# Placement of short extra matmuls in TensorE's stream, in a two-block transformer kernel

## The chip, the cores and the metric

The kernel runs on one core of one Trainium2 chip. The metric is the device time of one execution in microseconds (us). The core's engines are TensorE (PE, matmuls), VectorE (DVE), ScalarE (ACT), GpSimd (POOL) and SyncE (SP, which issues the loads). "PEld" in a profile is TensorE's weight load, which overlaps its matmuls.

## The reference

256 tokens of width 1024, everything in float32. Two blocks of two layers each, run one after the other:

- first block: a layer with MLA attention (16 heads) and one with an mLSTM mixer (4 heads), each followed by a squared-ReLU MLP of width 4096;
- second block: in each of two layers a SwiGLU MLP of width 2816, a mixer (a gated short convolution in the first, sparse attention with compressed, selected and windowed keys in the second), and a second SwiGLU MLP.

```python
for i in range(DEPTH):                      # first block, DEPTH = 2
    hn = rms_norm(x, norm_mix[i])
    y = mla_mixer(hn, ...) if i == 0 else mlstm_mixer(hn, ...)
    x = x + y
    x = x + sqrelu_mlp(rms_norm(x, norm_ffn[i]), ffn_w1[i], ffn_w2[i])
for i in range(DEPTH):                      # second block
    if i == 1: kv = shared_kv(h, ...)
    h = h + 0.5 * swiglu_ffn(rmsnorm(h, ffn1_norm[i]), ffn1_w_in[i], ffn1_w_out[i])
    hn = rmsnorm(h, mix_norm[i])
    h = h + (short_conv_mixer(hn, ...) if i == 0 else nsa_mixer(hn, ..., kv))
    h = h + 0.5 * swiglu_ffn(rmsnorm(h, ffn2_norm[i]), ffn2_w_in[i], ffn2_w_out[i])
```

## The kernel before, in words

All weights are a stream of 518 tiles of 128x1024 (512 KB). A tile comes by DMA into one of four buffers `raw`, ScalarE rounds it to `w_hi` (L551), VectorE subtracts to get the rest, `w_lo` (L1018), and TensorE multiplies. The buffers go round: SP loads a tile into a buffer when VectorE has split the one before it.

Activations are split into high and low parts too and lie in `xs`, `hs` or `os`, features on the partitions and the 256 tokens beside one another. A product of one 128x128 weight chunk with one 128x256 activation chunk is therefore three matmuls into one PSUM bank, which `narrow_product` issues: L1731 (`w_hi` by high), L1732 (`w_hi` by low) and L1735 (`w_lo` by high). One weight tile holds eight such chunks, so a tile is 24 matmuls.

The stages come in this order: MLA with its output projection wo_a; up_0, down_0; mLSTM (mgate, mqk, mv, mo) and wo_m; up_1, down_1; glu_0, out_0; cin, cout; glu_1, out_1; kv and kvc; glu_2, out_2; the sparse attention (nq, ngate) and wo_n; glu_3, out_3.

- `feature` makes the stages dq, dkv, kr, mqk, kvc, up_*, glu_* and cin: one output of 128 features for each weight tile, eight chunks deep. Where `norm_` is given, `two` computes outputs 0 and 1 together, chunk by chunk, with the row sums of the norm (`sums`, L1750, L1753) ahead of the last chunk. Then come a head of outputs written out singly, with what `between` asks for behind some of them, and a rolled loop of eight outputs at a time.
- `residual` makes down_* (32 outputs of `up`, four tiles an output) and out_* (22 chunks, three tiles an output): output `o`, tile `j`, chunk `c`. It reads `hs`.
- `residual_one` makes wo_a, wo_m, cout and wo_n.

`odd_matmul` (L1724) multiplies a constant 128x128 matrix in plain float32 with 60 columns of ones, into the last columns of bank 7 that nobody reads. The profile shows it as two records of L1724. Its result is used nowhere. In the kernel before, up_0, up_1 and glu_3 (`odds=3`) issue three of them in output 2: inside the product of chunk 0 (between L1732 and L1735), behind chunk 2 and behind chunk 4. glu_0, cin and glu_1 (`odds=1`) issue one, behind the pair of outputs 0 and 1. Everything else issues none. The compression in glu_2 has one real matmul of the same form, `compressed_sums` (L2062), behind output 15.

Of the kernel before, what the change touches and what calls it, by code (L numbers as in the profile page):

```python
# [30 lines left out]
P = 128  # L31
# [3 lines left out]
KD = D // P  # L35
BLK = 8
TILE = BLK * P
RING = 4
# [13 lines left out]
FF1 = 4096 // P  # L52
FF2 = 2816 // P
# [83 lines left out]
def build(nc, x_in, tiles, vecs, rows, consts, rel_bias, w1c_k, w1c_v, w2c_k, w2c_v, y_out):  # L137
    ctx = ExitStack()
    with ctx:
        def sb(name, shape, dt=F32):  # L140
            return ctx.enter_context(nc.sbuf_tensor(name, shape, dt))
# [38 lines left out]
        xs = sb("xs", [P, KD * 2 * S], F32R)  # L180
# [10 lines left out]
        def bank(b, a=0, z=BANK, p=slice(None)):  # L191
            return psum[p, b * BANK + a:b * BANK + z]

        def const(name, a, z, p=slice(None)):
            at = CONST[name]
            return con[p, at + a:at + z]
# [1524 lines left out]
        def _(pe):  # L1721
            def odd_matmul(b=7):

                pe.matmul(bank(b, 448, 508), const("blockdiag", 0, P), ones[:, 0:60], start=True, stop=True)  # L1724

            def narrow_product(out_bank, lhs, k, src, first, last, inside=None):

                s, c = lhs
                x_hi, x_lo = src[:, k * 2 * S:k * 2 * S + S], src[:, k * 2 * S + S:(k + 1) * 2 * S]
                out = bank(out_bank, 0, S)  # L1730
                pe.matmul(out, w_hi[s][:, c:c + P], x_hi, start=first, stop=False)  # L1731
                pe.matmul(out, w_hi[s][:, c:c + P], x_lo, start=False, stop=False)  # L1732
                if inside:
                    inside()
                return pe.matmul(out, w_lo[s][:, c:c + P], x_hi, start=False, stop=last)  # L1735
# [17 lines left out]
                            ins = pe.matmul(bank(STAT, tb, tb + 1), ssq[:, tb * P:(tb + 1) * P], ones[:, 0:1], start=True, stop=True)  # L1753
                ins.then_inc(stat_done, 1)

            def feature(name, outs, xs_name, src=xs, norm_=None, between=None, norm_at=0, odds=0):


                between = between or {}
                t0, o0 = TILE0[name], OUT0[name]  # L1760

                def one(u, i=0, wait_x=False):
                    s, b = (t0 + u) % RING, (o0 + u) % 4
                    pe.wait_ge(lo_ready, i * 4 + (t0 + u + 1))
                    if not (isinstance(i, int) and o0 + u + 4 * i < 4):
                        pe.wait_ge(out_read, i * 4 + (o0 + u - 3))
                    for k in range(KD):
                        if wait_x:
                            pe.wait_ge(xs_ready, XS0[xs_name] + k + 1)
                        more = odds == 3 and u == 2 and isinstance(i, int) and i == 0  # L1770
                        ins = narrow_product(b, (s, k * P), k, src, k == 0, k == KD - 1, odd_matmul if more and k == 0 else None)
                        if more and k in (2, 4):
                            odd_matmul()
                    ins.then_inc(tile_done, 1)

                def two():

                    pe.wait_ge(lo_ready, t0 + 2)
                    pe.wait_ge(out_read, o0 + 1 - 3)
                    for k in range(KD):  # L1780
                        pe.wait_ge(xs_ready, XS0[xs_name] + k + 1)
                        if norm_ and k == KD - 1:
                            sums(norm_)
                        for u in range(2):
                            ins = narrow_product((o0 + u) % 4, ((t0 + u) % RING, k * P), k, src, k == 0, k == KD - 1)
                            if k == KD - 1:
                                ins.then_inc(tile_done, 1)

                head = outs if outs < 16 else outs % 8 or 8
                while head <= max([*between, 2 if odds else 0]):  # L1790
                    head += 8
                paired = norm_ is not None and outs > 1 and name != "dq"
                if paired:
                    two()
                if odds == 1:
                    odd_matmul()
                for u in range(2 if paired else 0, head):
                    one(u, 0, u == 0)
                    if u in between:
                        between[u]()  # L1800
                    if norm_ and not paired and u == norm_at:
                        sums(norm_)
                if head < outs:
                    with pe.Fori(0, (outs - head) // 8) as i:
                        for u in range(8):
                            one(head + u, i * 2)

            def residual(name, per, chunks, src, ready):

                t0, o0 = TILE0[name], OUT0[name]  # L1810
                for o in range(KD):
                    pe.wait_ge(out_read, o0 + o - 3)
                    for j in range(per):
                        t = t0 + o * per + j
                        pe.wait_ge(lo_ready, t + 1)
                        for k in range(min(BLK, chunks - j * BLK)):
                            c = j * BLK + k
                            if o == 0:
                                pe.wait_ge(*ready(c))
                            ins = narrow_product((o0 + o) % 4, (t % RING, k * P), c, src, c == 0, c == chunks - 1)  # L1820
                        ins.then_inc(tile_done, 1)

            def residual_one(name, src, ready, between=None):


                between = between or {}
                t0, o0 = TILE0[name], OUT0[name]

                def chunk(o, c):
                    if c == 0:  # L1830
                        pe.wait_ge(out_read, o0 + o - 3)
                        pe.wait_ge(lo_ready, t0 + o + 1)
                    ins = narrow_product((o0 + o) % 4, ((t0 + o) % RING, c * P), c, src, c == 0, c == KD - 1)
                    if c == KD - 1:
                        ins.then_inc(tile_done, 1)

                for c in range(KD):
                    pe.wait_ge(*ready(max(c, 1) if name == "wo_a" else c))
                    chunk(0, c)
                    chunk(1, c)  # L1840
                    if c in between:
                        between[c]()
                for o in range(2, KD):
                    for c in range(KD):
                        chunk(o, c)
# [177 lines left out]
            def swap_rows(o):  # L2023

                pe.wait_ge(c_flat_, o + 1)
                if o >= 2:
                    pe.wait_ge(c_swapped, o - 1)
                pe.matmul(bank(6 + o % 2, 0, S), c_turned_rows, c_flat[o], start=True, stop=True).then_inc(c_swap, 1)
# [182 lines left out]
            def warm(n, b=7):  # L2211

                for _ in range(n):
# [3 lines left out]
            warm(24)  # L2217
            mla()
            residual_one("wo_a", os_, after(xs_ready, XS0["o_a"]), {0: lambda: turn_outputs("o_a", o_tok, (a_o, H - 1), [6]), 1: lambda: turn_outputs("o_a", o_tok, (a_o, H), [7])})
            feature("up_0", FF1, "ffn_0", norm_="ffn_0", odds=3)  # L2220
            residual("down_0", FF1 // BLK, FF1, hs, after(hs_ready, hid0["up_0"]))
            mlstm()
            residual_one("wo_m", os_, after(xs_ready, XS0["o_m"]),
                         {3: lambda: turn_outputs("o_m", m_h, (m_gated, 2), [4, 5, 6]),
                          4: lambda: turn_outputs("o_m", m_h, (m_gated, 2), [7])})
            feature("up_1", FF1, "ffn_1", norm_="ffn_1", odds=3)
            residual("down_1", FF1 // BLK, FF1, hs, after(hs_ready, hid0["up_1"]))
            feature("glu_0", 2 * FF2, "pre_0", norm_="pre_0", odds=1)
            residual("out_0", FF2_TILES, FF2, hs, after(hs_ready, hid0["glu_0"]))
            feature("cin", 3 * KD, "mid_0", norm_="mid_0", odds=1)  # L2230
            residual_one("cout", hs, after(hs_ready, hid0["cin"]))
            feature("glu_1", 2 * FF2, "post_0", norm_="post_0", odds=1)
            residual("out_1", FF2_TILES, FF2, hs, after(hs_ready, hid0["glu_1"]))
            nsa_kv()
            feature("glu_2", 2 * FF2, "pre_1", os_, between={2: lambda: swap_rows(3), 6: keys_turned, 10: compress, 13: compressed, 15: compressed_sums})
            residual("out_2", FF2_TILES, FF2, hs, after(hs_ready, hid0["glu_2"]))
            nsa()
            residual_one("wo_n", os_, after(xs_ready, XS0["o_n"]), {c: lambda c=c: turn_outputs("o_n", no_tok, (n_oo, 1), [c + 4]) for c in range(KD - 4)})
            feature("glu_3", 2 * FF2, "post_1", norm_="post_1", odds=3)
            residual("out_3", FF2_TILES, FF2, hs, after(hs_ready, hid0["glu_3"]))  # L2240


# [105 lines left out]
```

## Time and profile before

| | |
|---|---|
| time, median of 3 runs | 1556.84 us (1556.03 to 1557.47) |
| the profiled execution | 1556.84 us, span of the trace 1555.1 us |
| PE busy | 1541.5 us, 99% |
| DVE busy, ACT busy | 1041.9 us (67%), 849.8 us (55%) |
| granted TensorE clock | 1.00 over the span |
| HBM read | 278 MB, 180 GB/s |

Matmuls are pipelined: one lasts longer in the trace than the time from its start to the next start, so a busy PE may run at different paces. The start times of the timeline are in us from the start of the span; L1731 and so on are lines of the kernel. A window's count (x) includes instructions that overlap its edges.

### The profile page before, as it was taken

To read this page: it belongs to the slowest core of one execution; us is meant where nothing else is said; L and a number is where in the kernel's file an instruction comes from. 1 tells how busy PE (TensorE), PEld (TensorE's weight loads), DVE (VectorE), ACT (ScalarE), POOL (GpSimd) and SP (SyncE) were. 2 spreads that over 40 slices of the span, in tenths; PEclk is the share of its full clock that TensorE was granted. 3 is DMA by queue.
4 is the path that set the end of the run, shared out by engine and by line. 5 is a ranking of instruction groups with operands and counts; after the bars stand their busy time and mean duration, and the time that the engine had idled before them with its cause. 6 is when DMAs were issued, how large, how long until landed. Compare 5 with 4: busy or idle time off the path is not lost.

```text
span 1555.1 us, 35183 instructions
## 1 busy us (share of the span) xinstructions
PE 1541.5 (99%) x12856; PEld 1502.0 (97%) x12856; DVE 1041.9 (67%) x1751; ACT 849.8 (55%) x1301; POOL 124.1 (8%) x123
## 2 busy tenths in 40 slices
PE   9999999999999999999999999999999999999999
PEld 8899999988999999999999999989999988999999
DVE  7677765643876557666787766678576656676664
ACT  6776554546665445445445555556555547655543
POOL 1830000036000000000000000000000032200000
PEclk9999999999999999999999999999999999999999
DMA  7246666554566566666666666656566981065564
GB/s 242 71 123 193 197 192 197 169 168 148 183 194 197 188 199 190 195 193 202 193 204 191 200 191 192 211 179 208 188 192 195 229 210 55 15 203 190 192 201 149
DMA packets 80784, 281.02 MB, mean 181 GB/s; under 512 B 8880, under 2 KB 12464, under 8 KB 80688
## 3 DMA queue, kind: packets, MB, share of 16 engines
q1 hardware_dynamic: 76800, 274.78, 56.2%
q10 hardware_dynamic: 3888, 4.85, 1.7%
q8 instruction: 73, 1.20, 0.3%
q14 instruction: 23, 0.19, 0.0%
HBM read 278.03 MB, written 1.57 MB: 180 GB/s over the span
## 4 chain that ended last, share of the span: by engine, by line
PE 93%; DVE 4%; DMA 2%; ACT 1%; issue 1%; SPq 0%; DVEq 0%; ACTq 0%
PE psum L1731 27%; PE psum L1735 27%; PE psum L1732 27%; DMA raw<-tiles 2%; PE psum L1862 2%; PE psum L1864 2%; PE psum L1863 2%; PE psum L2151 1%; PE psum L2102 1%; DVE w_lo L1018 1%; PE psum L2135 1%; PE psum L2049 0%; ACT w_hi L551 0%; PE psum L1926 0%; PE psum L1916 0%
## 5 line engine op out<-in xcount | busy, mean ns | idle before, releaser
L551 ACT ACTIVATE w_hi<-raw 128x1024 fp32r<-128x1024 f32 x518 | 547.1, 1058 | 483.1 <-PE psum L1735 423.6
L1018 DVE TENSOR_TENSOR w_lo<-raw,w_hi 128x1024 fp32r<-128x1024 f32 x484 | 592.2, 1224 | 247.7 <-ACT w_hi L551 247.1
L1731 PE MATMUL psum<-xs,w_hi 128*128 128x256 f32 x1928 | 535.8, 278 | 2.1 <-DVE w_lo L1018 2.1
L1735 PE MATMUL psum<-xs,w_lo 128*128 128x256 f32 x1928 | 533.0, 276 | 0.0
L1732 PE MATMUL psum<-xs,w_hi 128*128 128x256 f32 x1928 | 532.8, 276 | 0.0
L1731 PEld LDWEIGHTS psum<-xs,w_hi 128*128 128x128 f32 x1928 | 361.9, 188 | 3.1 <-DVE w_lo L1018 2.5
L1732 PEld LDWEIGHTS psum<-xs,w_hi 128*128 128x128 f32 x1928 | 361.9, 188 | 0.3
L1735 PEld LDWEIGHTS psum<-xs,w_lo 128*128 128x128 f32 x1928 | 361.8, 188 | 0.0
L1735 PE MATMUL psum<-hs,w_lo 128*128 128x256 f32 x1280 | 353.3, 276 | 0.0
L1731 PE MATMUL psum<-hs,w_hi 128*128 128x256 f32 x1280 | 353.3, 276 | 0.0
L1732 PE MATMUL psum<-hs,w_hi 128*128 128x256 f32 x1280 | 353.3, 276 | 0.0
L1731 PEld LDWEIGHTS psum<-hs,w_hi 128*128 128x128 f32 x1280 | 240.2, 188 | 0.0
L1735 PEld LDWEIGHTS psum<-hs,w_lo 128*128 128x128 f32 x1280 | 240.2, 188 | 0.0
L1732 PEld LDWEIGHTS psum<-hs,w_hi 128*128 128x128 f32 x1280 | 240.2, 188 | 0.0
L471 POOL TENSOR_TENSOR w_lo<-raw,w_hi 128x1024 fp32r<-128x1024 f32 x34 | 81.7, 2412 | 1175.5 <-ACT w_hi L551 1175.5
L1731 PE MATMUL psum<-os,w_hi 128*128 128x256 f32 x544 | 152.8, 281 | 0.6 <-DVE os L1212 0.6
L1732 PE MATMUL psum<-os,w_hi 128*128 128x256 f32 x544 | 151.3, 278 | 0.0
L1735 PE MATMUL psum<-os,w_lo 128*128 128x256 f32 x544 | 151.2, 278 | 0.0
L1731 PEld LDWEIGHTS psum<-os,w_hi 128*128 128x128 f32 x544 | 102.1, 188 | 1.1 <-DVE os L1212 0.9
L1732 PEld LDWEIGHTS psum<-os,w_hi 128*128 128x128 f32 x544 | 102.2, 188 | 0.1
L1735 PEld LDWEIGHTS psum<-os,w_lo 128*128 128x128 f32 x544 | 102.0, 187 | 0.0
L1041 DVE SCALAR_TENSOR_TENSOR xs<-x,vec,xs 128x256 fp32r<-128x256 f32 (+1 forms) x80 | 38.1, 482 | 54.0 <-ACT xs L565 54.0
(284 smaller groups left out, 1464.9 us busy)
## 6 DMA issues: line engine op xcount, KB each, us to landing
raw<-tiles SPq DMA_DIRECT2D x518, 512.0 KB, 4.3
bias<-bias_dram ACTq DMA_DIRECT2D x8, 256.0 KB, 8.6
x<-x_in SPq DMA_DIRECT2D x4, 256.0 KB, 5.2
w1c_all<-w1c_k ACTq DMA_DIRECT2D x4, 256.0 KB, 4.3
w1c_all<-w1c_v ACTq DMA_DIRECT2D x4, 256.0 KB, 5.8
y_out<-x SPq DMA_DIRECT2D x8, 128.0 KB, 3.5
con<-consts SPq DMA_DIRECT2D x1, 771.0 KB, 8.9
bias_dram<-bias_row ACTq DMA_DIRECT2D x1, 512.0 KB, 7.1
```

Of the source, the lines that this page charges most:

```text
L471: pool.tensor_tensor(w_lo[s][:, :], raw[s][:, :], w_hi[s][:, :].bitcast(F32), ALU.subtract).then_inc(lo_ready, 1)
L551: act.activation(w_hi[s][:, :], raw[s][:, :], ACT.Copy).then_inc(hi_ready, 1)
L1018: dve.tensor_tensor(w_lo[s][:, :], raw[s][:, :], hi_of(w_hi[s][:, :]), ALU.subtract).then_inc(lo_ready, 1)
L1041: dve.scalar_tensor_tensor(out=dst, in0=src, scalar=gain, in1=hi_of(hi), op0=ALU.mult, op1=ALU.subtract).then_inc(xs_ready, 1)
L1731: pe.matmul(out, w_hi[s][:, c:c + P], x_hi, start=first, stop=False)
L1732: pe.matmul(out, w_hi[s][:, c:c + P], x_lo, start=False, stop=False)
L1735: return pe.matmul(out, w_lo[s][:, c:c + P], x_hi, start=False, stop=last)
L1862: pe.matmul(out, x_hi, w_hi[s][:, col:col + 512], start=c == 0, stop=False)
L1863: pe.matmul(out, x_hi, w_lo[s][:, col:col + 512], start=False, stop=False)
L1864: ins = pe.matmul(out, x_lo, w_hi[s][:, col:col + 512], start=False, stop=c == chunks - 1)
L2102: return pe.matmul(bank(n_bank[2 * e + br], at_, at_ + k1), n_qTa[rows, k * S + q0:k * S + q1], kT[rows, key0:key0 + k1], start=True, stop ...
L2135: ins = pe.transpose(bank(4 + br, n * P, (n + 1) * P), n_p[e][:, col:col + P], ident)
```

## The change

The option `odds` of `feature` goes. In its place `inside` names a function to call within the product of chunk 4 of a given output (between L1732 and L1735), beside `between`, which calls one behind an output.

- up_0, up_1, glu_0, cin, glu_1 and glu_3: three short matmuls each, inside chunk 4 of output 2, behind output 2 and behind output 3.
- glu_2: three, in the same way, at outputs 16, 16 and 17, into bank 4.
- every `residual` stage (down_0, down_1, out_0 to out_3): three in output 0, inside the product of chunk 4, behind tile 0 and behind tile 1.

```diff
-            def feature(name, outs, xs_name, src=xs, norm_=None, between=None, norm_at=0, odds=0):
+            def feature(name, outs, xs_name, src=xs, norm_=None, between=None, norm_at=0, inside=None):
-                between = between or {}
+                between, inside = between or {}, inside or {}
...
-                        more = odds == 3 and u == 2 and isinstance(i, int) and i == 0
-                        ins = narrow_product(b, (s, k * P), k, src, k == 0, k == KD - 1, odd_matmul if more and k == 0 else None)
-                        if more and k in (2, 4):
-                            odd_matmul()
+                        ins = narrow_product(b, (s, k * P), k, src, k == 0, k == KD - 1, inside.get(u) if k == 4 else None)
...
-                while head <= max([*between, 2 if odds else 0]):
+                while head <= max(between, default=0):
                     head += 8
...
-                if odds == 1:
-                    odd_matmul()
...
-                            ins = narrow_product((o0 + o) % 4, (t % RING, k * P), c, src, c == 0, c == chunks - 1)
+                            ins = narrow_product((o0 + o) % 4, (t % RING, k * P), c, src, c == 0, c == chunks - 1,
+                                                 odd_matmul if (o, c) == (0, 4) else None)
                         ins.then_inc(tile_done, 1)
+                        if o == 0 and j < 2:
+                            odd_matmul()
...
-            feature("up_0", FF1, "ffn_0", norm_="ffn_0", odds=3)
+            feature("up_0", FF1, "ffn_0", norm_="ffn_0", between={2: odd_matmul, 3: odd_matmul}, inside={2: odd_matmul})
...
-            feature("glu_0", 2 * FF2, "pre_0", norm_="pre_0", odds=1)
+            feature("glu_0", 2 * FF2, "pre_0", norm_="pre_0", between={2: odd_matmul, 3: odd_matmul}, inside={2: odd_matmul})
...
-            feature("glu_2", 2 * FF2, "pre_1", os_, between={2: lambda: swap_rows(3), 6: keys_turned, 10: compress, 13: compressed, 15: compressed_sums})
+            feature("glu_2", 2 * FF2, "pre_1", os_, between={2: lambda: swap_rows(3), 6: keys_turned, 10: compress, 13: compressed, 15: compressed_sums, 16: lambda: odd_matmul(4), 17: lambda: odd_matmul(4)}, inside={16: lambda: odd_matmul(4)})
```

up_1 and glu_3 change like up_0, cin and glu_1 like glu_0.

## Rows read from the trace of the kernel before

**Rows 1.** The page: busy time of the engines, and the chain by engine.
```profile
PE 1541.5 (99%) x12856; PEld 1502.0 (97%) x12856; DVE 1041.9 (67%) x1751; ACT 849.8 (55%) x1301; POOL 124.1 (8%) x123
...
PE 93%; DVE 4%; DMA 2%; ACT 1%; issue 1%; SPq 0%; DVEq 0%; ACTq 0%
```

**Rows 2.** Waits of PE: us in total, times, longest.
```profile
PE psum L2096 <- DVE arena L1605: 2.2, 2, 1.9
PE psum L1731 <- DVE w_lo L1018: 2.1, 2, 1.6
```

**Rows 3.** Windows, PE alone: window, us, PE busy (count), granted clock, DMA share, GB/s.
```profile
101.00:123.00 22.00, 22.00 (x189) 1.00 0.65 168
130.00:290.00 160.00, 160.00 (x1414) 1.00 0.63 196
...
1125.00:1250.00 125.00, 125.00 (x1106) 1.00 0.74 206
...
1385.00:1545.00 160.00, 160.00 (x1414) 1.00 0.61 198
```

**Rows 4.** Line L1735 on `hs`, whole span: ns min/median/max, first and last start.
```profile
L1735 PE MATMUL psum<-hs,w_lo x1280: 276/276/278, 207.9 to 1551.7; 128*128 128x256 f32 x183
```

**Rows 5.** Timeline of PE in glu_0: start, duration (us).
```profile
587.60 0.28 PE L1735 MATMUL psum<-xs,w_lo 128*128 128x256 f32 x1
587.71 0.33 PE L1724 MATMUL psum<-ones,con 128*128 128x60 f32 x2
...
588.05 0.28 PE L1732 MATMUL psum<-xs,w_hi 128*128 128x256 f32 x1
```

**Rows 6.** Timeline of PE in up_0, output 2.
```profile
125.55 0.32 PE L1724 MATMUL psum<-ones,con 128*128 128x60 f32 x2
...
125.89 0.28 PE L1731 MATMUL psum<-xs,w_hi 128*128 128x256 f32 x1
...
126.46 0.28 PE L1735 MATMUL psum<-xs,w_lo 128*128 128x256 f32 x1
126.58 0.33 PE L1724 MATMUL psum<-ones,con 128*128 128x60 f32 x2
126.71 0.37 PE L1731 MATMUL psum<-xs,w_hi 128*128 128x256 f32 x1
126.92 0.28 PE L1732 MATMUL psum<-xs,w_hi 128*128 128x256 f32 x1
...
127.39 0.28 PE L1735 MATMUL psum<-xs,w_lo 128*128 128x256 f32 x1
```

**Rows 7.** Timeline of PE in glu_3, output 2.
```profile
1377.15 0.28 PE L1732 MATMUL psum<-xs,w_hi 128*128 128x256 f32 x1
...
1377.61 0.28 PE L1731 MATMUL psum<-xs,w_hi 128*128 128x256 f32 x1
...
1378.20 0.28 PE L1735 MATMUL psum<-xs,w_lo 128*128 128x256 f32 x1
...
1378.66 0.28 PE L1732 MATMUL psum<-xs,w_hi 128*128 128x256 f32 x1
...
1379.13 0.28 PE L1735 MATMUL psum<-xs,w_lo 128*128 128x256 f32 x1
...
1379.58 0.28 PE L1732 MATMUL psum<-xs,w_hi 128*128 128x256 f32 x1
```

**Rows 8.** Groups by line, 124.95 to 125.42 (up_0): busy us, mean ns.
```profile
L1735 PE MATMUL psum<-xs,w_lo 128*128 128x256 f32 x2 | 0.6, 280 | 0.0
```

**Rows 9.** Groups by line, 587.38 to 587.65 (glu_0).
```profile
L1731 PE MATMUL psum<-xs,w_hi 128*128 128x256 f32 x1 | 0.3, 280 | 0.0
```

**Rows 10.** Groups by line, 1376.65 to 1377.12 (glu_3, ahead of the first L1724).
```profile
L1731 PE MATMUL psum<-xs,w_hi 128*128 128x256 f32 x2 | 0.6, 280 | 0.0
```

**Rows 11.** Groups by line, 1377.86 to 1378.18 (glu_3, behind the first L1724).
```profile
L1735 PE MATMUL psum<-xs,w_lo 128*128 128x256 f32 x1 | 0.3, 280 | 0.0
```

**Rows 12.** Timeline of PE in glu_2, behind output 15.
```profile
1121.13 0.33 PE L2062 MATMUL psum<-arena,con 128*128 128x60 f32 x2
```

More of the change, by code:

```diff
@@ L2225, in _ @@
                           4: lambda: turn_outputs("o_m", m_h, (m_gated, 2), [7])})
-            feature("up_1", FF1, "ffn_1", norm_="ffn_1", odds=3)
+            feature("up_1", FF1, "ffn_1", norm_="ffn_1", between={2: odd_matmul, 3: odd_matmul}, inside={2: odd_matmul})
             residual("down_1", FF1 // BLK, FF1, hs, after(hs_ready, hid0["up_1"]))
-            feature("glu_0", 2 * FF2, "pre_0", norm_="pre_0", odds=1)
+            feature("glu_0", 2 * FF2, "pre_0", norm_="pre_0", between={2: odd_matmul, 3: odd_matmul}, inside={2: odd_matmul})
             residual("out_0", FF2_TILES, FF2, hs, after(hs_ready, hid0["glu_0"]))
-            feature("cin", 3 * KD, "mid_0", norm_="mid_0", odds=1)
+            feature("cin", 3 * KD, "mid_0", norm_="mid_0", between={2: odd_matmul, 3: odd_matmul}, inside={2: odd_matmul})
             residual_one("cout", hs, after(hs_ready, hid0["cin"]))
-            feature("glu_1", 2 * FF2, "post_0", norm_="post_0", odds=1)
+            feature("glu_1", 2 * FF2, "post_0", norm_="post_0", between={2: odd_matmul, 3: odd_matmul}, inside={2: odd_matmul})
             residual("out_1", FF2_TILES, FF2, hs, after(hs_ready, hid0["glu_1"]))
             nsa_kv()
-            feature("glu_2", 2 * FF2, "pre_1", os_, between={2: lambda: swap_rows(3), 6: keys_turned, 10: compress, 13: compressed, 15: compressed_sums})
+            feature("glu_2", 2 * FF2, "pre_1", os_, between={2: lambda: swap_rows(3), 6: keys_turned, 10: compress, 13: compressed, 15: compressed_sums, 16: lambda: odd_matmul(4), 17: lambda: odd_matmul(4)}, inside={16: lambda: odd_matmul(4)})
             residual("out_2", FF2_TILES, FF2, hs, after(hs_ready, hid0["glu_2"]))
@@ L2238, in _ @@
             residual_one("wo_n", os_, after(xs_ready, XS0["o_n"]), {c: lambda c=c: turn_outputs("o_n", no_tok, (n_oo, 1), [c + 4]) for c in range(KD - 4)})
-            feature("glu_3", 2 * FF2, "post_1", norm_="post_1", odds=3)
+            feature("glu_3", 2 * FF2, "post_1", norm_="post_1", between={2: odd_matmul, 3: odd_matmul}, inside={2: odd_matmul})
             residual("out_3", FF2_TILES, FF2, hs, after(hs_ready, hid0["glu_3"]))
```

## Prediction

> **What bounds the kernel now.** I read the page first. TensorE (PE) is busy for 1541.5 of 1555.1 us, VectorE for 67% and ScalarE for 55%, and 93% of the chain that ended last is PE [rows 1]. The view of waits says the same: the longest total wait of PE for another engine is 2.2 us, the one for a split weight tile 2.1 us [rows 2]. So PE's own stream sets the end; time added to it adds to the span, and nearly nothing beside it can hide it.
>
> But "busy" can't say how fast the stream runs. I therefore counted PE's matmuls in stretches that hold only the products of `narrow_product` (256 columns each). A row counts about two matmuls that straddle the edges of its window. From 130 to 290 us that gives 160/(1414-2) = 0.1133 us from one start to the next; from 101 to 123 us it gives 22/(189-2) = 0.1176 us [rows 3]. The granted clock is 1.00 in both, the level of 2.4 GHz. So the same instructions run at two paces, 0.0043 us (3.8%) apart. I call them fast and slow. Each has its own duration of one matmul as well: 276 ns when fast [rows 4], up to 280 ns when slow [rows 8 to 11]. From the end of the short matmuls of up_0 to the end of down_0, and likewise in up_1/down_1, glu_0/out_0, cin/cout, glu_1/out_1, the rest of glu_2/out_2 and glu_3/out_3, the pace is fast. In particular the 1280 matmuls of L1735 on `hs`, which are those of every `down`, `out` and `cout` stage, last 276 ns in the median and 278 at most [rows 4]: no such stage has a slow stretch today.
>
> **What a short matmul does, from the timeline.** The order in time around the existing short ones (L1724) shows that they switch the pace.
>
> - glu_0, one of them, between L1735 and the next L1731: slow before, fast after [rows 5].
> - up_0, three: after L1732 (slow to fast), after an L1735 (fast to slow), after an L1735 (slow to fast). The five steps from 125.89 to 126.46 take 0.114 each, the four from 126.92 to 127.39 0.1175 [rows 6].
> - glu_3, three at the same places: slow, slow, slow, and fast only after the third. The five steps from 1377.61 to 1378.20 still take 0.118, the four from 1378.66 to 1379.13 too; from 1385 us on the pace is 160/1412 = 0.1133 [rows 3, 7].
>
> So it is no plain toggle. In the slow pace one of the three matmuls of a product lasts 280 ns and the others a nanosecond or two less, and which one it is differs: L1735 ahead of up_0's first short matmul, L1731 ahead of the one in glu_0 and of glu_3's first, L1735 again after glu_3's first [rows 8 to 11]. All the cases fit one rule: if the 280 ns matmul is the one right behind the insertion, the pace becomes fast; otherwise it becomes slow (or stays so) with the 280 ns matmul moved to just behind the insertion. A 60-column matmul of the compression (L2062) did the same at 1121.13, so that glu_2 runs fast from its tile 16 on today: 125/1104 = 0.1132 [rows 3, 12].
>
> The new train is: inside chunk 4 (ahead of L1735), after the tile (ahead of L1731), after the next tile (ahead of L1731). By the rule it ends fast from every start: the first leaves "fast" or "280 at L1735", the second then always "280 at L1731", the third always "fast". I don't expect the change to lose the fast pace; it can't win it either, because every stage that it touches has it already, and the slow stretches (wo_a, mLSTM's projections, wo_m, kvc and the first 16 tiles of glu_2, wo_n) lie outside it or ahead of its trains.
>
> **The sum, from the profiled execution (1556.84 us, which is also the median of the runs).** What is left is the price.
>
> One short matmul: in glu_3, L1732 at 1377.15 to L1732 at 1379.58 is 2.43 us and holds 15 steps, three for each of five chunks [rows 7]. At 0.1176 they make 1.76, so the three cost 0.67 over the slow pace, 0.22 each. The one in glu_0 agrees: 588.05-587.60 = 0.45 for two steps, less 0.235 [rows 5]. The fast-to-slow one: 126.92-126.46 = 0.46, the same [rows 6].
>
> 1. Six residual stages (down_0, down_1, out_0 to out_3), all new: three short ones 0.67. Between the first and the last 34 matmuls (10 to the end of the first tile, 24 of the second) and the two steps spanning the last one turn slow: 36 x 0.0043 = 0.155. Together 0.82 each, 4.9 us.
> 2. glu_2, new, in a stretch that L2062 had made fast: same shape, 0.82.
> 3. glu_0, cin, glu_1: one short one becomes three (+0.45), and the pace turns fast two tiles later (48 x 0.0043 = 0.21): 0.66 each, 2.0 us.
> 4. up_0, up_1: three before and after, spread wider. Of the 50 steps behind the pair of tiles, 12 are slow before and 42 after: 30 x 0.0043 = 0.13 each, 0.26 us.
> 5. glu_3: 17 of the 50 slow before, all after: 33 x 0.0043 = 0.14 us.
>
> Sum 4.9 + 0.8 + 2.0 + 0.26 + 0.14 = 8.1 us, with 27 more short matmuls (39 for 12). 1556.84 + 8.1 = **1564.9 us**, 0.5% slower.
>
> The edits that I cost at nothing: the bank (4 or 7) and the `inside` plumbing, which issue nothing. DMA, VectorE and ScalarE get no new work, and their ring of four weight tiles is fed with slack (VectorE 67% busy). If that cover were gone, PE would wait at a tile start; a delay of PE only gives them more time. Conversely, up to the 2.1 us that PE waits for split tiles today [rows 2] could swallow some of the delay. That is the low bound: 1564.9 - 2.1 = 1562.8. What queues behind a short matmul is only the next product; the tile's release to the DMA ring comes 0.22 us later.
>
> What isn't seen before is an insertion inside a product while the pace is fast. Its price is bounded by the nearest rows: 0.22 and slow afterwards (as the other fast-to-slow one), or 0.22 and still fast for the 10 matmuls to the next one, which saves 7 x 10 x 0.0043 = 0.3 us. I take the first. Below nothing isn't possible where the pace is already fast.
>
> **The rivals.**
>
> *A (not slower): a short matmul pays only for its columns.* With the stream already fast, its two records of 60 columns might slip in at the pace of the others: 120/256 x 0.1133 = 0.053 us, 27 of them 1.4 us, with the pace kept: 1558.3 us, within 0.2%. It decides below 3.1/27 = 0.115 us for one. For it: two records start only 0.13 us before the product after them [rows 6]. Against it: in up_0 the one put into a fast stream took 0.46 for two steps like the others, twice the deciding price. Chance 0.04. The Trainium skill, page TensorE: Matmul & The Clock Gate, section "Wait — 56ns, not 53.3ns?", says that starts come no closer than about 25 ns however few the columns; an estimate from that page is 27 x 2 x 0.025 = 1.4 us, 1558.2 us.
>
> *B (slower, but by less): the new short matmuls cost their time and don't move the pace.* 27 x 0.22 = 6.0 us, 1562.8 us. Against it: up_0's second one made a fast stream slow [rows 6]; for it: none was seen inside a product of a fast stream. Chance 0.02. The Trainium skill, page TensorE: Matmul & The Clock Gate, same section, gives one start-to-start time at the full clock, N/2.4 plus about 2.5 ns, or 109 ns for 256 columns; by that rule an insertion never moves the pace, while the trace has two paces, 113.3 and 117.6 ns, at one granted clock.
>
> *C: a train that starts fast ends slow.* If inserting inside a product from the fast pace left the 280 ns matmul at L1731 rather than L1735, the second would give fast and the third slow. Then down_0 and down_1 run their other 718 matmuls slow (3.1 us each), the four out stages 478 each (2.1), glu_2's rest 624 (2.7): 6.2 + 8.4 + 2.7 = 17 us more, less out_2, which would then start slow and be mended: 15, or 1580 us. For it: this transition is in no row. Against it: the rule fits every one that is, and glu_3 shows that inside from slow leaves it at L1735. A plain toggle would give about the same time, and glu_3 speaks against it. Chance 0.05.
>
> *D: one or two stages only end slow*, because at some place the steps between the insertions are disturbed (a wait for a tile or a bank at the tile's boundary). 2.1 to 3.1 us each: 1567 to 1571 us. The one in glu_0 sits at such a boundary and works, as do those in cin and glu_1. Chance 0.05.
>
> *E: a train mends more than its own stage*, say mLSTM's projections or wo_n, which are slow now. After down_0 these are 46 tiles of 24 matmuls (mgate 2, mqk 8, wo_m 8, kvc 4, 16 of glu_2, wo_n 8), 1104 x 0.0043 = 4.7 us: 1560.2 at best, still slower. Against it: at each of them row sums or other fp32 work comes between. Chance 0.02.
>
> **How the numbers follow.** My forecast has 0.82: 1564.9, with a range of its own from 1562.8 (some delay swallowed) to 1566. A has 0.04, B 0.02, C 0.05, D 0.05, E 0.02. The range of 1562.5 to 1570 takes in the forecast, B and most of D, 0.88 or so. 0.2% is 3.1 us, about what a measurement of this kernel can tell from no change. Slower by more: forecast, B, C, D and E, 0.94 to 0.96; I say 0.94. Within: A and a little more absorption, 0.05. Faster: 0.01, for something that no row shows.
>
> **What the profile after would show.** 78 records of the short matmul in place of 24; in each residual stage the durations rise from 276 to up to 280 ns from chunk 4 to the end of chunk 15 of the first output and are back at 276 from then on; each of these stages 0.8 us longer; glu_2 0.8 us longer behind tile 16; glu_0, cin, glu_1 0.66 us longer; PE busy by about 8 us more; the median over the matmuls on `hs` still 276 ns. I am wrong if that median goes to 279 (C), if a short one costs under 0.12 us (A), if a new train leaves the pace as it is (B), or if unprofiled executions don't run at the paces of this profile.

## The result, and the profile after

The changed kernel takes 1565.29 us (1564.33 to 1567.98, 4 runs) against 1556.43 us for the kernel before (1555.81 to 1557.47, 4 runs): ratio 1.0057, 95% interval 1.0044 to 1.0069. It is 8.9 us slower; 8.1 were forecast. The profiled execution took 1565.57 us, its span is 1563.8 us.

The page of the changed kernel, the lines that answer to [rows 1]:

```profile
PE 1551.1 (99%) x12910; PEld 1511.7 (97%) x12910; DVE 1042.3 (67%) x1751; ACT 849.8 (54%) x1301; POOL 123.9 (8%) x123
...
PE 95%; DVE 3%; ACT 1%; issue 0%; DMA 0%; SPq 0%; ACTq 0%; DVEq 0%
```

PE is busy for 9.6 us more with 54 more matmul records; VectorE and ScalarE do what they did. The view of single lines (ns min/median/max) has the short matmuls, 78 records for 24, and L1735 on `hs`, which answers to [rows 4]:

```profile
L1724 PE MATMUL psum<-ones,con x78: 213/244/274, 126.8 to 1506.0; 128*128 128x60 f32 x78
```

```profile
L1735 PE MATMUL psum<-hs,w_lo x1280: 276/276/366, 207.9 to 1560.5; 128*128 128x256 f32 x183
```

The median is still 276 ns: the residual stages are fast except close to their trains. Only the maximum is new, the matmul right behind an insertion. (An insertion is one short matmul, a train the two or three that stand together.) Windows of PE in the changed kernel, behind the trains of up_0, down_0 and out_3, read as [rows 3]:

```profile
130.00:205.00 75.00, 75.00 (x664) 1.00 0.64 201
215.00:299.00 84.00, 84.00 (x743) 1.00 0.60 193
...
1507.00:1560.00 53.00, 53.00 (x471) 1.00 0.53 175
```

75/662 = 0.1133, 84/741 = 0.1134 and 53/469 = 0.1130 us: the fast pace, within a matmul or two of the count. The timeline of PE around the third insertion of down_0's train shows the return to it:

```profile
213.58 0.28 PE L1735 MATMUL psum<-hs,w_lo 128*128 128x256 f32 x1
213.70 0.33 PE L1724 MATMUL psum<-ones,con 128*128 128x60 f32 x2
...
214.04 0.28 PE L1732 MATMUL psum<-hs,w_hi 128*128 128x256 f32 x1
214.15 0.28 PE L1735 MATMUL psum<-hs,w_lo 128*128 128x256 f32 x1
214.26 0.28 PE L1731 MATMUL psum<-hs,w_hi 128*128 128x256 f32 x1
```

From 213.58 to 214.04 are two steps of 0.46 in all, as in [rows 5 to 7], and then 0.11 each.

The norms' row sums (L1750) are marks to measure stages by: they stand ahead of the last chunk of the first pair of outputs, so 42 product matmuls into up_0, mgate, up_1, glu_0 and so on. From the mark in up_0 to the one in mgate is nearly all of up_0, all of down_0 and those 42. First the kernel before, then the changed one, in the timeline of PE; the marks lie in up_0, mgate, glu_0 and cin:

```profile
124.18 0.59 PE L1750 MATMUL psum<-ssq,ones 128*128 128x256 f32 x2
299.43 0.59 PE L1750 MATMUL psum<-ssq,ones 128*128 128x256 f32 x2
...
586.57 0.59 PE L1750 MATMUL psum<-ssq,ones 128*128 128x256 f32 x2
766.78 0.59 PE L1750 MATMUL psum<-ssq,ones 128*128 128x256 f32 x2
```

```profile
124.03 0.59 PE L1750 MATMUL psum<-ssq,ones 128*128 128x256 f32 x2
300.29 0.59 PE L1750 MATMUL psum<-ssq,ones 128*128 128x256 f32 x2
...
588.41 0.59 PE L1750 MATMUL psum<-ssq,ones 128*128 128x256 f32 x2
770.10 0.59 PE L1750 MATMUL psum<-ssq,ones 128*128 128x256 f32 x2
```

up_0/down_0 went from 175.25 to 176.26 us, glu_0/out_0 from 180.21 to 181.69. All stages by such marks (glu_2 from L2062 to the last product of out_2, glu_3 from its mark to the last product of out_3):

| stretch | forecast, us | measured, us |
|---|---|---|
| up_0, down_0 | 0.13 + 0.82 | 1.00 |
| up_1, down_1 | 0.13 + 0.82 | 1.00 |
| glu_0, out_0 | 0.66 + 0.82 | 1.49 |
| cin, cout | 0.66 | 0.66 |
| glu_1, out_1 | 0.66 + 0.82 | 1.49 |
| rest of glu_2, out_2 | 0.82 + 0.82 | 1.65 |
| glu_3, out_3 | 0.14 + 0.82 | 0.93 |
| sum | 8.1 | 8.2 |

up_0 and glu_3 are a little off because their trains met another slow pace than the forecast had them meet. Which of the three matmuls of a product lasts 280 ns I call the phase of the slow pace. PE's groups by line in the changed kernel, ahead of the train in up_0 (125.9 to 126.75) and in glu_3 (1385.6 to 1386.35):

```profile
L1731 PE MATMUL psum<-xs,w_hi 128*128 128x256 f32 x3 | 0.8, 280 | 0.0
```

```profile
L1735 PE MATMUL psum<-xs,w_lo 128*128 128x256 f32 x3 | 0.8, 280 | 0.0
```

In the trace of before it was L1735 in up_0 and L1731 in glu_3 [rows 8, 10]; in experiment 1, whose kernel is the same as before up to down_0, it was L1731 in up_0 too. From L1735 the first insertion gives ten fast matmuls, from L1731 none: up_0 got 38 slow steps more in place of 30 (0.16 us for 0.13), glu_3 25 in place of 33 (0.11 for 0.14). So the phase at one place isn't the same in every execution, and the train ended fast all the same.

The span grew by 8.7. Of the rest, 0.65 us came in the sparse attention, which the change doesn't touch and where the clock was granted at half for 3.4 us (last section), and the part ahead of up_0 was 0.15 us shorter.

### The profile page after: what moved, and what is told of

Its sections match the earlier page's. It is cut to its first block, busy times and chain, and to the rows that moved or that the text cites. A ratio compares the mean times of both kernels' runs of the same rounds, so it can differ in the third digit from the quotient of the medians.

```text
span 1563.8 us, 35291 instructions
## 1 busy us (share of the span) xinstructions
PE 1551.1 (99%) x12910; PEld 1511.7 (97%) x12910; DVE 1042.3 (67%) x1751; ACT 849.8 (54%) x1301; POOL 123.9 (8%) x123
## 4 chain that ended last, share of the span: by engine, by line
PE 95%; DVE 3%; ACT 1%; issue 0%; DMA 0%; SPq 0%; ACTq 0%; DVEq 0%
PE psum L1731 27%; PE psum L1732 27%; PE psum L1735 27%; PE psum L1860 2%; PE psum L1862 2%; PE psum L1861 2%; PE psum L2149 1%; PE psum L2100 1%; PE psum L2133 1%; PE psum L2047 0%; DVE w_lo L1018 0%; PE psum L1924 0%; PE psum L1724 0%; PE psum L1914 0%; PE psum L2094 0%
## 5 line engine op out<-in xcount | busy, mean ns | idle before, releaser
L1731 PE MATMUL psum<-xs,w_hi 128*128 128x256 f32 x1928 | 536.3, 278 | 1.7 <-DVE w_lo L1018 1.6
L1735 PE MATMUL psum<-xs,w_lo 128*128 128x256 f32 x1928 | 533.5, 277 | 0.0
L1732 PE MATMUL psum<-xs,w_hi 128*128 128x256 f32 x1928 | 533.0, 276 | 0.0
L1731 PEld LDWEIGHTS psum<-xs,w_hi 128*128 128x128 f32 x1928 | 362.0, 188 | 2.7 <-DVE w_lo L1018 2.1
L1732 PEld LDWEIGHTS psum<-xs,w_hi 128*128 128x128 f32 x1928 | 361.9, 188 | 0.3
L1735 PEld LDWEIGHTS psum<-xs,w_lo 128*128 128x128 f32 x1928 | 362.0, 188 | 0.0
L1731 PE MATMUL psum<-hs,w_hi 128*128 128x256 f32 x1280 | 354.6, 277 | 0.0
L1735 PE MATMUL psum<-hs,w_lo 128*128 128x256 f32 x1280 | 354.0, 277 | 0.0
L1732 PE MATMUL psum<-hs,w_hi 128*128 128x256 f32 x1280 | 353.5, 276 | 0.0
L1731 PEld LDWEIGHTS psum<-hs,w_hi 128*128 128x128 f32 x1280 | 240.3, 188 | 0.0
L1735 PEld LDWEIGHTS psum<-hs,w_lo 128*128 128x128 f32 x1280 | 240.3, 188 | 0.0
L1732 PEld LDWEIGHTS psum<-hs,w_hi 128*128 128x128 f32 x1280 | 240.3, 188 | 0.0
L1731 PE MATMUL psum<-os,w_hi 128*128 128x256 f32 x544 | 153.0, 281 | 0.6 <-DVE os L1212 0.6
L1735 PE MATMUL psum<-os,w_lo 128*128 128x256 f32 x544 | 151.4, 278 | 0.0
L1732 PE MATMUL psum<-os,w_hi 128*128 128x256 f32 x544 | 151.3, 278 | 0.0
L1731 PEld LDWEIGHTS psum<-os,w_hi 128*128 128x128 f32 x544 | 102.1, 188 | 1.1 <-DVE os L1212 0.9
L1732 PEld LDWEIGHTS psum<-os,w_hi 128*128 128x128 f32 x544 | 102.2, 188 | 0.1
L1735 PEld LDWEIGHTS psum<-os,w_lo 128*128 128x128 f32 x544 | 102.0, 188 | 0.0
```

## The experiments

**1. The residual stages' trains alone.** To the kernel before is added

```diff
+ ins = narrow_product(..., c == chunks - 1, odd_matmul if (o, c) == (0, 4) else None)
  ins.then_inc(tile_done, 1)
+ if o == 0 and j < 2:
+     odd_matmul()
```

> The kernel before plus the residual part of the change alone: three short matmuls in output 0 of each of the six residual stages. Theory (0.22 us for each short matmul, and 36 steps between them slow by 0.0043 us): 6 x 0.82 = 4.9 us over the kernel before, ratio 1.0032. Rival (the insertions cost their time, the pace does not move): 18 x 0.22 = 4.0 us. Rival (a train begun fast ends slow): about 19 us.

Measured: 1562.36 against 1557.40 us, ratio 1.0029 (1.0017 to 1.0041), 5.0 us. In the trace each stretch with a residual stage is longer by 0.83 to 0.85 us. That fits 0.82 and not 0.66 (three times 0.22 with the pace kept); the total alone would not tell these two apart.

**2. The feature stages alone.** The changed kernel with `residual` as before and glu_2 without its three.

> The changed kernel with the trains of the residual stages and of glu_2 taken out, so only up_0, up_1, glu_0, cin, glu_1, glu_3 differ from before. Theory: 3 x 0.66 + 2 x 0.13 + 0.14 = 2.4 us over the kernel before, ratio 1.0015. Rival (insertions cost their time, the pace does not move): 6 x 0.22 = 1.3 us.

Measured: 1559.47 against 1557.40 us, ratio 1.0014 (1.0005 to 1.0024), 2.1 us; by the marks 0.66 for each of glu_0, cin and glu_1, 0.17 and 0.13 for up_0 and up_1, 0.11 for glu_3. Runs 1 and 2 with glu_2's 0.82 make 7.9 us by the times and 5.0 + 2.4 + 0.8 = 8.2 by the marks, as in the changed kernel: the parts add up.

**3. No short matmul at all.**

```diff
- feature("up_0", ..., odds=3)
+ feature("up_0", ...)
```

and so in up_1, glu_0, cin, glu_1 and glu_3.

> The kernel before without any short matmul. Theory (they switch the pace): the stages from up_0, up_1, glu_0, cin, glu_1 and glu_3 up to the next fp32 matmul stay slow, some 8260 steps x 0.0043 = 35.5 us, less 12 x 0.22 = 2.6: 33 us slower, ratio 1.021. Rival (the pace of a stage has another cause, say the stage's own operands, and the insertions are only a cost): 2.6 us faster. glu_2 should be fast from its tile 16 on in both, by its own 60-column matmul.

Measured: 1591.55 against 1557.40 us, ratio 1.0219 (1.0203 to 1.0235), 34 us. Windows of PE, the second one in glu_2 behind L2062:

```profile
130.00:290.00 160.00, 160.00 (x1361) 1.00 0.56 191
...
1155.00:1280.00 125.00, 125.00 (x1105) 1.00 0.72 210
1410.00:1580.00 170.00, 170.00 (x1446) 1.00 0.58 190
```

160/1359 = 0.1177 and 170/1444 = 0.1177, but 125/1103 = 0.1133 where L2062 did the work. So matmuls that compute nothing used are worth 34 us, and the pace is theirs.

**4. One insertion inside a product of a fast stream**, in each residual stage: the addition of experiment 1 without its last two lines.

> The kernel before plus one short matmul, inside the product of chunk 4 of output 0, in each residual stage. Theory (from the fast pace one insertion gives the slow pace with the 280 ns matmul at L1735, and nothing mends it): 2 x 754 + 4 x 514 = 3564 steps x 0.0043 = 15.3 us, plus 6 x 0.22 = 1.3: 16.7 us slower, ratio 1.0107. Rival (inside a product of a fast stream it leaves the pace as it is): 1.3 us slower.

Measured: 1575.14 against 1557.40 us, ratio 1.0116 (1.0100 to 1.0131), 17.7 us. This is the transition that no row of before showed. PE's groups by line in down_0, 215 to 300 us:

```profile
L1735 PE MATMUL psum<-hs,w_lo 128*128 128x256 f32 x237 | 66.4, 280 | 0.0
L1731 PE MATMUL psum<-hs,w_hi 128*128 128x256 f32 x236 | 65.8, 279 | 0.0
L1732 PE MATMUL psum<-hs,w_hi 128*128 128x256 f32 x236 | 65.8, 279 | 0.0
```

Slow, with the longest matmul right behind the place of the insertion, in all six stages. Nothing mends it by itself: it lasts into the next stage, so that the stretches are 3.8 us longer with a down stage and 2.5 to 2.7 with an out stage, 17.8 in all.

**5. Two insertions, three matmuls apart.** As 4, with `(o, c) in ((0, 4), (0, 5))`.

> The kernel before plus two short matmuls in each residual stage, inside the products of chunks 4 and 5 of output 0, so three product matmuls apart. Theory (the first moves the 280 ns matmul to L1735, the second stands ahead of an L1735 and brings the fast pace back): 6 x (0.44 + 5 x 0.0043) = 2.8 us slower, ratio 1.0018; the rest of each residual stage at 276 ns. Rival (only an insertion ahead of L1731 brings the fast pace back): some 15 us more, 18 us slower.

Measured: 1576.28 against 1556.49 us, ratio 1.0127 (1.0112 to 1.0142), 19.8 us: the rival's size. My rule failed here: the second insertion stood where it should have mended. Timeline of PE, an L1731 and an L1732 left out:

```profile
208.83 0.32 PE L1724 MATMUL psum<-ones,con 128*128 128x60 f32 x2
208.96 0.37 PE L1735 MATMUL psum<-hs,w_lo 128*128 128x256 f32 x1
...
209.41 0.33 PE L1724 MATMUL psum<-ones,con 128*128 128x60 f32 x2
```

A window of PE behind it in the same kernel:

```profile
215.00:298.00 83.00, 83.00 (x707) 1.00 0.56 187
```

83/705 = 0.1177, slow.

**6. Two insertions, six matmuls apart**, `(o, c) in ((0, 4), (0, 6))`.

> Two short matmuls in each residual stage as in the run with chunks 4 and 5, but inside chunks 4 and 6, six product matmuls apart in place of three. Theory (the rule holds only once the slow pace has settled behind an insertion, and three matmuls are too few): fast again behind the second, 6 x (0.44 + 8 x 0.0043) = 2.8 us over the kernel before, ratio 1.0018. Rival (two insertions at the same kind of place in a row never mend a stream that was fast, or only those ahead of L1731 do): about 19 us, as the run with chunks 4 and 5.

Measured: 1560.28 against 1557.41 us, ratio 1.0017 (1.0008 to 1.0027), 2.9 us. The same window:

```profile
215.00:298.00 83.00, 83.00 (x735) 1.00 0.60 196
```

83/733 = 0.1132: fast. One chunk more between the two is worth 17 us. Places inside a product mend as well as those ahead of L1731, but not three matmuls behind an insertion that ended a long fast stretch. (In up_0 of the kernel before, too, six matmuls behind such an insertion are enough [rows 6]; four and five were not tried.) A train of two so placed costs a fast stretch 0.48 us in place of 0.82.

**7. One record in place of two.** As 4, but `pe.matmul(bank(7, 448, 508), w_hi[s][:, k * P:(k + 1) * P], src[:, c * 2 * S:c * 2 * S + 60], start=True, stop=True)` is inserted.

> As the run with one short matmul inside chunk 4, but the inserted one multiplies the same weights and activations as the product (60 columns, one record in the trace, not plain float32 with two). Theory 1 (any extra matmul moves the pace): slow for the rest of each residual stage, 15.3 us plus about 6 x 0.11. Theory 2 (it takes the two records of a plain float32 matmul): the pace stays fast, 0.3 to 0.7 us slower.

Measured: 1574.62 against 1556.49 us, ratio 1.0115 (1.0101 to 1.0130), 18.1 us, and L1735 at 280 ns again. Timeline of PE:

```profile
209.07 0.28 PE L1732 MATMUL psum<-hs,w_hi 128*128 128x256 f32 x1
209.19 0.19 PE L1821 MATMUL psum<-hs,w_hi 128*128 128x60 f32 x1
209.21 0.37 PE L1735 MATMUL psum<-hs,w_lo 128*128 128x256 f32 x1
209.42 0.28 PE L1731 MATMUL psum<-hs,w_hi 128*128 128x256 f32 x1
```

Two steps take 0.35 us, 0.12 over the fast pace, where a plain float32 insertion costs 0.22 to 0.23. The effect isn't tied to a plain float32 matmul. Whether the cheap form also mends was not tried.

**8. 128 columns in place of 60**, `bank(7, 384, 512)` and `ones[:, 0:128]`, else as 4.

> As the run with one short matmul inside chunk 4, but with 128 columns of ones in place of 60. Theory 1 (the insertion as such moves the pace): slow for the rest of each residual stage with the 280 ns matmul at L1735, 15.3 us plus 6 x 0.28, 17 us slower. Theory 2 (its length in time decides): another phase, or the fast pace kept, then under 2 us slower.

Measured: 1587.78 against 1556.49 us, ratio 1.0202 (1.0187 to 1.0217), 31.3 us, 14 more than the larger of the two theories. Groups by line in down_0, 215 to 300 us:

```profile
L1732 PE MATMUL psum<-hs,w_hi 128*128 128x256 f32 x236 | 66.1, 280 | 0.0
L1731 PE MATMUL psum<-hs,w_hi 128*128 128x256 f32 x236 | 65.8, 279 | 0.0
L1735 PE MATMUL psum<-hs,w_lo 128*128 128x256 f32 x236 | 65.8, 279 | 0.0
```

Slow too, but with the long matmul at L1732: of the two widths tried, "right behind the insertion" holds for 60 columns only. It isn't the time that the insertion takes, for that is the same. Timeline of PE:

```profile
209.05 0.28 PE L1732 MATMUL psum<-hs,w_hi 128*128 128x256 f32 x1
...
209.51 0.28 PE L1731 MATMUL psum<-hs,w_hi 128*128 128x256 f32 x1
```

Two steps take 0.46 us with 128 columns as with 60. So a short matmul does not pay by its columns, which rival A took for granted. And the next stages suffer. Windows of PE in glu_0 and glu_1:

```profile
600.00:700.00 100.00, 100.00 (x851) 1.00 0.58 194
880.00:980.00 100.00, 100.00 (x852) 1.00 0.56 192
```

100/849 = 0.1178, and 100/850 = 0.1176: their single insertion no longer hits. In the kernel before the stage ahead of it ended fast, in experiment 4 slow with the 280 ns matmul at L1735, and it hit both times; here the stage ahead ends slow in another phase. That the phase is handed on through the row sums is my reading of these three cases; a run for it alone was not made. In cin the last L1731 ahead of the insertion lasts 284 ns, the longest around, and by the letter of the rule the insertion should have mended: six matmuls behind row sums the rule isn't safe. By the marks glu_0/out_0 is 7.2 us longer, cin/cout 3.4 and glu_1/out_1 7.1, where experiment 4 has 2.7, 0.0 and 2.5.

**9. The changed kernel without the insertion inside the product**, so trains of two behind the tiles.

```diff
- feature("up_0", ..., between={2: odd_matmul, 3: odd_matmul}, inside={2: odd_matmul})
+ feature("up_0", ..., between={2: odd_matmul, 3: odd_matmul})
```

and so everywhere, `residual` too.

> The changed kernel without the short matmul inside the product, everywhere (13 fewer), so that each train is the two behind the tiles. Theory (from the state 280 at L1731, which glu_0 and glu_1 start from, the first brings the fast pace and the second takes it away): glu_0/out_0 and glu_1/out_1 run slow but for two tiles, 2 x 6.3 us, and each of up_0, up_1, glu_3 too if it happens to start there; less 13 x 0.22 = 2.9: from about 10 us slower than the changed kernel, in levels of 6 us, so at least 15 us over the kernel before. Rival (two are enough): 2.9 us faster than the changed kernel, 5.5 over the kernel before.

Measured: 1578.50 (1576.94 to 1584.95) against 1557.41 us, ratio 1.0147 (1.0122 to 1.0172). That is 21 us over the kernel before. Windows in down_1, cin, glu_1 and glu_3:

```profile
510.00:590.00 80.00, 80.00 (x681) 1.00 0.56 185
785.00:860.00 75.00, 75.00 (x639) 1.00 0.58 191
880.00:980.00 100.00, 100.00 (x885) 1.00 0.62 195
1400.00:1510.00 110.00, 110.00 (x936) 1.00 0.59 191
```

0.1178, 0.1177, 0.1133, 0.1178. By the marks up_1/down_1 and glu_3/out_3 are 6.8 us longer than before and cin/cout 3.5. The levels of 6 us were right, and up_1 and glu_3 could be slow by the theory; but glu_0 and glu_1, which it had slow for certain, ended fast, and cin slow, so that the total came near the forecast by luck. Groups by line just ahead of the trains in glu_0 (596.0 to 597.8) and cin (777 to 779):

```profile
L1732 PE MATMUL psum<-xs,w_hi 128*128 128x256 f32 x6 | 1.7, 280 | 0.0
```

```profile
L1731 PE MATMUL psum<-xs,w_hi 128*128 128x256 f32 x6 | 1.7, 280 | 0.0
```

glu_0 did not start from the phase that I had assumed, with the slow down_1 ahead of it. With the phases that the trace shows, the rule gives the right end for every train of this run: slow from L1731, fast from L1732, L1735 or the fast pace. One of the four executions took 1584.95 us, a level of 6 us higher; it has no trace. The insertion inside is what makes the train independent of its start: in the traces of the changed kernel and of experiment 2 trains of three started from L1731, from L1735 and from the fast pace, and all ended fast. None started from L1732.

**10. Insertions only where the start is known, and earlier.** wo_a, wo_m and wo_n get a close train in output 2 (inside chunk 0, behind chunks 0 and 1), up_0, up_1 and glu_3 one behind the pair, mqk one behind mgate, glu_2 three single ones.

> A version for speed by the rule. The train of three stands in the slow stages ahead of up_0, up_1 and glu_3 instead (output 2 of wo_a, wo_m, wo_n, close together), where the start is not known; up_0, up_1 and glu_3 then begin from a known state and get one, behind the pair, as glu_0 does; mqk gets one behind mgate; glu_2 gets three single ones at the place its slow phase asks for (ahead of L1732 at outputs 3 and 11, ahead of L1735 at output 7). Theory: 7 more short matmuls +1.5 us, about 890 steps fast instead of slow, -3.8 us: 2.3 us faster than the kernel before, ratio 0.9985. Rival (the phases are not reproducible from run to run, so single insertions miss): one or more of these stages slow in the profile and up to 3 us slower for each.

Measured: 1559.72 against 1556.49 us, ratio 1.0016 (1.0007 to 1.0026): 3.2 us slower, where 2.3 faster was forecast, and the rival came true. With the clock granted in full throughout it stood at 1554.6 us once and at 1559.5 to 1559.9 five times, and this was expected of a second profile:

> The same kernel as the early version, profiled again, because at the full clock its times stood at 1554.6 us once and at 1559.5 to 1559.9 us in five runs. Theory: the single insertions miss in some executions. If this one is near 1559.7 or above, the trace shows one stage (up_0, up_1 or glu_3 with its residual) at 279 to 280 ns per matmul. Rival (another 5 us, say more half-clock windows): every such stage at 276 ns and more time at the half clock.

That execution took 1561.18 us. Its windows in glu_2, ahead of L2062, and in glu_2/out_2 behind it:

```profile
1115.00:1120.00 5.00, 5.00 (x46) 1.00 0.61 210
1122.00:1255.00 133.00, 133.00 (x1132) 1.00 0.68 203
```

133/1130 = 0.1177, 1200 matmuls slow, 5.2 us; in the profile of the first run the stretch was fast. All of up_0, up_1 and glu_3 were fast: the single insertions missed, as the theory had it, but in a stage that I hadn't named. The two profiles, of one and the same kernel, differ from the first of the three on: it made 95 matmuls fast in this execution and none in the other. Here the third left the stage slow in another phase, the compression's own matmuls behind output 13 then made it fast (5/44 = 0.114 ahead of L2062), and L2062 took the pace away. mqk's insertion, six matmuls behind the row sums, had no effect in either profile.

**11. The same without glu_2's three, and mqk's behind its output 1.**

```diff
  for c in range(KD):
-     chunk(o, c)
+     more = name != "cout" and o == 2
+     chunk(o, c, odd_matmul if more and c == 0 else None)
+     if more and c < 2:
+         odd_matmul()
...
- feature("mqk", 8, "mix_1")
+ feature("mqk", 8, "mix_1", between={1: odd_matmul})
...
- feature("up_0", ..., odds=3)
+ feature("up_0", ..., odds=1)
```

> The early version without its three insertions in glu_2, whose own 60-column matmul they had turned against it, and with mqk's single one behind its output 1 in place of behind mgate, so that the pace has settled. Theory: 5 more short matmuls than before (+1.1 us), 136 x 3 steps of wo_a, wo_m, wo_n, 144 of mqk and 35 in up_0, up_1, glu_3 fast instead of slow (587 x 0.0043 = 2.5): 1.4 us faster than the kernel before, ratio 0.9991; all of up, glu_2, out_2 and glu_3 at 276 ns, and no second level of times 5 us higher. Rival (a single insertion misses in some executions here too): a level some 6 us higher, a median at or over that of the kernel before.

Measured: 1555.18 (1553.32 to 1556.89) against 1557.34 us, ratio 0.9987 (0.9978 to 0.9996), with no second level. Windows in wo_a, wo_m and glu_2/out_2:

```profile
104.00:122.00 18.00, 18.00 (x161) 1.00 0.59 185
...
391.00:409.00 18.00, 18.00 (x161) 1.00 0.52 177
1130.00:1250.00 120.00, 120.00 (x1061) 1.00 0.70 214
```

18/159 = 0.1132 in wo_a, which ran at 0.1176 before [rows 3]. It is faster than both kernels, by little: 0.1% under the kernel before, 0.7% under the changed one (by the two ratios). The theory's 1.4 us (0.9991) lies in the interval; it counted 5 more short matmuls than before where there are 4 (32 records for 24), which makes it 1.6. The trains in wo_a, wo_m and wo_n have only one and three matmuls between their members. In the three profiles of experiments 10 and 11 all nine of them started in a slow stretch and ended fast.

## Why the prediction was right

- **PE sets the end** held: what was added to PE's stream reached the total.
- **Two paces, 0.0043 us apart, switched by short matmuls**: shown by experiment 3 (34 us, windows at 0.1177) and 4.
- **The rule** foretold that each train of the changed kernel ends fast, and it foretold experiments 4 and 6. What it can't foretell is the phase ahead of a train, which changes from one execution to the next (up_0 and glu_3 above, experiments 9 and 10). By 8, it isn't safe six matmuls behind row sums that follow a slow stage. It also needed two corrections that the changed kernel doesn't touch: it doesn't hold three matmuls behind an insertion that ended a long fast stretch (5 against 6), and of 60 and 128 columns it is only with 60 that the new phase is right behind the insertion (8). The trains of the change have 10 and 24 matmuls between, enough by these runs.
- **The price**, 0.22 us for each short one and the slow steps between and ahead of them, was right to 0.05 us a stage, as the table shows; experiments 1 and 2 split it. That the total of 8.9 us lies 0.8 over the forecast is mostly not the trains, which measure 8.2. A (1.4 us) and B (6.0 us) are out by it, A also by experiment 8, where 128 columns cost what 60 do; B by experiment 1's 0.83 a stage, though not by its total.
- **C** was the transition in question and fell with experiment 4: it leaves the longest matmul at L1735. **D** and **E**: no stage of the changed kernel ended slow, and mqk and wo_n stayed slow.
- **"Up to 2.1 us could be swallowed"**: no. The waits for split tiles (2.1 us before, 1.6 after) lie in MLA, ahead of the change. A wait of 0.6 us at the start of the sparse attention, for the row sums (L1753), is gone after, but the half-clock stretch that came there cost more.

What I had not forecast is the spread: the four runs of the changed kernel span 3.65 us. The kernel before spreads as much, 1555.11 to 1559.10 us in the 17 runs beside experiments 5, 7, 8 and 10.

## What to carry to other kernels

When PE looks 99% busy, divide a window by its count of matmuls: the same instructions may run at two paces at one granted clock, and a cheap extra matmul may switch them. First find out which stages are slow; a remedy in stages that are fast already is a pure cost, here 8 us of 1557. Where the phase ahead isn't reproducible, use a train that ends well from every start, and put it once, as early as it can stand; where the stretch ahead may be fast, leave room between its members (six matmuls did, three did not). Where the phase is known, one insertion does. And look for matmuls of the kernel's own that switch the pace back.

## What the runs showed of the hardware that I had not expected

- A 60-column matmul put in between products of three 256-column ones switches between 113.3 and 117.7 ns per matmul at a granted clock of 1.00, and the state lasted for up to 1584 matmuls, until the next foreign matmul (experiment 3). Why the pace has these levels, and why the slow one has three phases (the 280 ns matmul first, second or third of a product), stays open; the runs show when it switches, not what in the engine does.
- The clock was granted at half for none, one or two stretches of 3.4 us early in the sparse attention: none in the traces of before and of experiments 4 and 11, two in 1, 3, 6 and the first of 10, one in the others. The changed kernel's five executions with mean clock 1.000 took 1564.1 to 1564.8 us, four with mean clock 0.999 took 1565.4 to 1565.8, two with 0.998 took 1567.0 and 1568.0; the kernel before spreads in the same way. Windows of PE in the changed kernel, ahead of and in such a stretch:

```profile
1293.90:1303.90 10.00, 7.86 (x65) 1.00 0.13 48
1303.90:1307.30 3.40, 3.40 (x20) 0.50 0.00 0
```

PE had been busy for 7.9 of 10 us, waiting for softmax work in between; 0.50 is the level of 1.2 GHz. But waiting isn't all: where there were two stretches, PE had been busy throughout ahead of the first, though with small matmuls. Windows of experiment 1:

```profile
1283.30:1293.30 10.00, 10.00 (x70) 1.00 0.47 160
1293.30:1296.70 3.40, 3.40 (x18) 0.51 0.00 0
```

What decides it stays open. This sets most of the spread between runs, and at 1.5 us or so each it is nearly as large as two of the trains. The Trainium skill, page TensorE: Matmul & The Clock Gate, section "What's actually happening", has these two levels; its section "Wait — 56ns, not 53.3ns?" has a single start-to-start time at the full clock, where the trace has two.
